# Folding a norm gain into a weight split and moving two pieces of work in a recurrent layer (HGRN) of a one-core kernel

## The reference, cut to what matters

```python
def hgrn2_mixer(h, w_in, lower_bound, out_norm, w_out, first_layer):
    q, f, i, g = jnp.split(h @ w_in, ..., axis=-1)     # four sections of 1024 columns
    q = jax.nn.silu(q)
    log_f = jax.nn.log_sigmoid(f32)                    # first layer
    k = -jnp.expm1(log_f)
    ...
    # by chunks of 64 tokens, each head: G = cumsum(log_f)
    #   attn[t, s] = sum_k q[t, k] * k[s, k] * exp(G[t, k] - G[s, k])   for s <= t
    #   o = attn @ i + (q * exp(G)) @ state
    o = rms_norm_2(o, out_norm) * jax.nn.silu(g.reshape(B, S, HGRN_HEADS, HGRN_DV).astype(jnp.float32))
    return o.reshape(B, S, HGRN_D_VAL).astype(h.dtype) @ w_out
```

## Time and profile before

| | us |
|---|---|
| median of 3 runs | 1095.07 |
| lowest, highest | 1093.2, 1097.18 |
| the profiled execution's own time | 1091.74 |
| its span | 1089.9 |
| PE, PEld busy | 1035.1 (95%), 847.1 (78%) |
| DVE, ACT, POOL busy | 780.1 (72%), 506.3 (46%), 111.9 (10%) |

### The profile page before, as it was taken

One profiled execution on the slowest core, in us unless ns is written; L12 is line 12 of the kernel. 1 busy time (PEld: TensorE's weight loads), 2 busy tenths in 40 slices (PEclk: granted clock), 3 DMA queues, 4 the chain that ended last, 5 costly groups with the idle time before them and its releaser, 6 DMA issues.

```text
span 1089.9 us, 16320 instructions
## 1 busy us (share of the span) xinstructions
PE 1035.1 (95%) x6217; PEld 847.1 (78%) x6217; DVE 780.1 (72%) x1023; ACT 506.3 (46%) x645; POOL 111.9 (10%) x137
## 2 busy tenths in 40 slices
PE   6998999999989999698999999999999989999998
PEld 5887777878867888587778888877878877888886
DVE  5776767786666878887898787788846786454554
ACT  5536364444544584453344343335547735443441
POOL 1000000000001000581300000000850200000000
PEclk9999999999999999899999999999999999999999
DMA  8975358698726977004399898954413064655641
GB/s 314 337 277 203 116 191 323 241 371 297 256 86 216 343 262 246 17 2 162 103 328 342 294 309 284 322 200 151 135 52 135 2 193 141 207 160 188 212 152 58
DMA packets 126959, 224.12 MB, mean 206 GB/s; under 512 B 4824, under 2 KB 58296, under 8 KB 126904
## 3 DMA queue, kind: packets, MB, share of 16 engines
q1 hardware_dynamic: 125936, 220.90, 58.0%
q0 software_dynamic: 656, 2.36, 0.8%
q10 hardware_dynamic: 312, 0.10, 0.0%
HBM read 222.30 MB, written 1.05 MB: 205 GB/s over the span
## 4 chain that ended last, share of the span: by engine, by line
PE 80%; DVE 13%; issue 3%; ACT 3%; DMA 1%; SPq 0%; POOL 0%; DVEq 0%; ACTq 0%; PEldq 0%
PE psum L1732 76%; DVE adaacc L1133 3%; DVE wlo L1107 2%; DVE arena L1174 2%; ACT whi L706 2%; PE psum L2372 1%; PE psum L2202 1%; DVE arena L1220 1%; DMA raw<-in_attn_w_qkv 1%; DVE arena L1435 1%; DVE gain_b L1435 1%; PE psum L2061 1%; DVE adaw L1382 1%; DVE res L1225 0%; PE psum L2289 0%
## 5 line engine op out<-in xcount | busy, mean ns | idle before, releaser
L1107 DVE TENSOR_TENSOR wlo<-raw,whi 128x2048 fp32r<-128x2048 f32 (+1 forms) x166 | 330.5, 2006 | 132.1 <-ACT whi L706 132.0
L1732 PE MATMUL psum<-whi,xhi 128*128 128x512 f32 x880 | 350.5, 398 | 11.3 <-DVE xlo L1182 10.4
L706 ACT CAST whi<-raw 128x2048 fp32r<-128x2048 f32 (+1 forms) x166 | 278.2, 1684 | 165.4 <-PE psum L1732 141.3
L1732 PE MATMUL psum<-whi,xlo 128*128 128x512 f32 x880 | 343.9, 391 | 0.0
L1732 PE MATMUL psum<-wlo,xhi 128*128 128x512 f32 x880 | 342.2, 390 | 0.0
L1732 PEld LDWEIGHTS psum<-whi,xhi 128*128 128x128 f32 x880 | 165.8, 188 | 47.8 <-issue 14.2
L1732 PEld LDWEIGHTS psum<-whi,xlo 128*128 128x128 f32 x880 | 165.6, 188 | 35.4
L1732 PEld LDWEIGHTS psum<-wlo,xhi 128*128 128x128 f32 x880 | 166.0, 189 | 32.3
L1133 DVE SCALAR_TENSOR_TENSOR adaacc<-adaw,cact,adaacc 128x512 f32<-128x512 f32 x196 | 147.3, 752 | 7.0 <-DMA adaw<-in_ada_w 0.2
L1732 PE MATMUL psum<-whi,hhi 128*128 128x512 f32 x304 | 120.2, 395 | 4.2 <-DVE wlo L1107 2.7
L1732 PE MATMUL psum<-whi,hlo 128*128 128x512 f32 x304 | 118.5, 390 | 0.0
(11 more groups left out here) (278 smaller groups left out, 1013.6 us busy)
## 6 DMA issues: line engine op xcount, KB each, us to landing
adaw<-in_ada_w SPq DMA_DIRECT2D x48, 1024.0 KB, 5.6
raw<-in_ffn_w_in SPq DMA_DIRECT2D x88, 512.0 KB
raw<-in_ffn_w_out SPq DMA_DIRECT2D x44, 512.0 KB
raw<-in_w_up SPq DMA_DIRECT2D x16, 1024.0 KB
raw<-in_w_down SPq DMA_DIRECT2D x16, 1024.0 KB
raw<-in_hgrn_w_in SPq DMA_DIRECT2D x16, 1024.0 KB
raw<-in_attn_w_qkv SPq DMA_DIRECT2D x12, 1024.0 KB
adaw<-in_kv_ada_w SPq DMA_DIRECT2D x8, 1024.0 KB, 6.8
```

The lines of the kernel that those rows point to most:

```text
L706: sc.copy(whi[:, s, 0:width], raw[:, s, 0:width]).then_inc(hi_ready[s], 1)
L1107: ve.tensor_tensor(wlo[:, s, 0:width], raw[:, s, 0:width], whi[:, s, 0:width].bitcast(F32), ALU.subtract).then_inc(lo_ready[s], 1)
L1732: return te.matmul(dst, lhsT, rhs, start=start, stop=stop, skip_group_check=open_)
```

## The change

Three edits, all in the HGRN layer.

1. The gain is no longer multiplied into the gate (`gains` and its two calls are gone). It is multiplied into the rows of `w_out`. A slot's partition p holds rows whose channel is p, so the gain is a column with one value for each partition: `onb`, now 128 x 1 in `stat`, loaded by a DMA of one column. For item `Q_HOUT` (four slots) ScalarE's high split is a multiply by this column and VectorE's low split is raw x column - high, one instruction of three operands. VectorE's and ScalarE's splits of this item wait for the column's DMA; VectorE's wait ahead of the heads is gone.
2. The diagonal sums move from the end of the projection into it: token tile 0 behind the third section's second eviction, tile 1 behind the fourth section's first eviction.
3. `outputs(HH - 1)` is called between part (0, 0) and part (0, 1) of the output projection.

```diff
-        onb = sb("onb", [P, DK])
+        onb = stat[:, 50:51]
...
-            gp.dma_start(onb[:], a["hgrn_out_norm_2"][0].partition_broadcast(P)).then_inc(norms_in, 16)
+            with nc.allow_non_contiguous_dma(reason="one column"):
+                gp.dma_start(onb, a["hgrn_out_norm_2"][0].rearrange("(p o) -> p o", o=1)).then_inc(norms_in, 16)
...
-                sc.copy(whi[:, s, 0:width], raw[:, s, 0:width]).then_inc(hi_ready[s], 1)
+                if isinstance(n, int) and n == Q_HOUT:
+                    act.wait_ge(norms_in, 16)
+                    sc.mul(whi[:, s, :], raw[:, s, :], onb).then_inc(hi_ready[s], 1)
+                else:
+                    sc.copy(whi[:, s, 0:width], raw[:, s, 0:width]).then_inc(hi_ready[s], 1)
...
-                ve.tensor_tensor(wlo[:, s, 0:width], raw[:, s, 0:width], whi[:, s, 0:width].bitcast(F32),
-                                 ALU.subtract).then_inc(lo_ready[s], 1)
+                if isinstance(n, int) and n == Q_HOUT:
+                    v.wait_ge(norms_in, 16)
+                    ve.scalar_tensor_tensor(wlo[:, s, :], raw[:, s, :], onb, whi[:, s, :].bitcast(F32), ALU.mult,
+                                            ALU.subtract).then_inc(lo_ready[s], 1)
+                else:
+                    ve.tensor_tensor(wlo[:, s, 0:width], raw[:, s, 0:width], whi[:, s, 0:width].bitcast(F32),
+                                     ALU.subtract).then_inc(lo_ready[s], 1)
...
-                        v.wait_ge(g_f, 2)
-                        for i in range(TT):
-                            chain(ve.tensor_tensor(qk, hin[:, 0, i, :], hk[:, i, :], ALU.mult))
-                            chain(ve.tensor_reduce(dg[:, i, :], qk.rearrange("p (h d) -> p h d", d=DK), AX, ALU.add))
                         q_part(0)
                     evac(Q_HIN + t, p, hin[:, sec, 1, p * 512:(p + 1) * 512])
+                    if (t, p) in ((N_HIN - 2, 1), (N_HIN - 1, 0)):
+                        i = t - (N_HIN - 2)
+                        v.wait_ge(g_f, 2)
+                        chain(ve.tensor_tensor(qk, hin[:, 0, i, :], hk[:, i, :], ALU.mult))
+                        chain(ve.tensor_reduce(dg[:, i, :], qk.rearrange("p (h d) -> p h d", d=DK), AX, ALU.add))
...
-            v.wait_ge(norms_in, 16)
...
-                    gains(4)
...
-                    gains(0)
...
                     part(0, 0)
+                    if second is not None:
+                        second()
                     part(0, 1)
...
-            outputs(HH - 1)
...
-            accumulate(Q_HOUT, 1, None, A_HOUT, 0, late_turn)
+            accumulate(Q_HOUT, 1, None, A_HOUT, 0, late_turn, second=lambda: outputs(HH - 1))
```

More of the change, by code:

```diff
@@ L1415, in gates_low @@
                                  ghi[:, :, b * 256:(b + 1) * 256].bitcast(F32), ALU.subtract).then_inc(g_lo, 1)
[L1417 to L1421, removed]
             def second(x, m):
@@ L1819, in project_tiles, with accumulate @@
                         project_part(n, 1, half, i, width)
-            def accumulate(n, turned, m=None, middle=None, gated=None, late=None, next_norm=None, early_high=False):
+            def accumulate(n, turned, m=None, middle=None, gated=None, late=None, next_norm=None, early_high=False, second=None):
                 def part(s, i):
```

## The result

The changed kernel took 1083.78 us (median of 4 runs, 1080.29 to 1084.53) against 1094.58 us (4 runs, 1093.2 to 1097.18): ratio 0.9894, interval 0.9873 to 0.9914. That is 10.8 us less; 11.4 were forecast. The profiled execution took 1084.53 us with a span of 1082.7, against 1089.9 before, a difference of only 7.2.

A forecast was written before the change was run, and what follows sets the result against it. The chain lies mostly on TensorE; in the HGRN layer, TensorE's waits for VectorE bound it. Terms 4.0 + 3.0 + 1.5 + 2.9 = 11.4 us took the median from 1095.07 to 1083.7, rounded to 1084; range 1080 to 1089.5.

The forecast's parts named there:

- Diagonal sums: End of the HGRN projection: pairs moved into VectorE's idle time let the first head's operand start 4.0 us earlier.
- the fold: Output-weight splits with the gain column: dearer VectorE splits cost the path 0.1 to 1.4 us, taken as 0.1.
- proportional price: VectorE's three-operand split: 752 ns for 512 elements scaled by length gives 3.01 us, 0.72 more per split.
- Gains: VectorE in the heads: removing the first gains call, slowed beside GpSimd, saves 3.0 us; the second call gives 0.
- Outputs: Last head: 12 projection matmuls before its output products remove TensorE's 1.50 us idle, so 1.5 us is gained.
- The last normed: VectorE's last normed, behind the last output products: 0.3 to 1.3 us later, with over 3 us to spare.
- The gate's weights: Weights for the gate after the output projection: if they land late, the outputs' gain is 0 to 1.5 us.
- Clock: TensorE in the heads: two slow-clock stretches vanish as idle shrinks, 1.35 + 1.55 = 2.9 us; bounds 0 and 4.2.
- The second stretch: TensorE at 462 to 468, granted clock 0.72, slowing scores and outputs: its removal gives 1.55 us.
- rival 2: Projection or head 1: one VectorE edit returns as a wait, 1089.1 or 1088.2 us; chance 0.10, both lost 0.05.
- rival 3: Heads, 440 to 490: TensorE stays at 1.2 GHz, 2 to 3 us per head, up to 1107.6; chance 0.03.
- Rival 1: Heads: the clock still falls, two stretches stay slow somewhere on the chain, 8.5 us gain remains, 1086.6; chance 0.20.

The follow-up runs named there:

- experiment 1: Kernel before with only the diagonal sums moved into the projection's third and fourth sections: 1089.22 us, ratio 0.995.
- experiment 2: Kernel before with only the output gain folded into the split of the output weights: 1092.52 us, ratio 0.9972.
- experiment 5: Kernel before with the first gains call cut to token tile 0, so heads 0 to 3 of tile 1 lack the gain: 1088.95 us, ratio 0.9958.
- experiment 3: Kernel before with only the last head's output products moved behind part (0, 0) of the output projection: 1092.65 us, ratio 0.998.
- experiment 4: Kernel before with 26 unread matmuls filling TensorE's idle time before head 1's exponents: 1092.93 us, ratio 0.9991.
- experiment 6: Changed kernel with 12 unread matmuls each before the last head's scores and the first MLP's modulation product: 1080.54 us, ratio to before 0.987.
- experiment 7: Changed kernel with both pairs of diagonal sums in the third section behind its second eviction: 1081.17 us, ratio to before 0.9876.
- experiment 8: Changed kernel with the edits of experiments 6 and 7 together: 1080.22 us, ratio to before 0.987.

## Why the prediction was right

**Diagonal sums: 4.0 forecast, 3.99 measured.** The hole before the third section's split took the first pair, as worked out; the first operand moved by 3.99 in the change and by 4.26 alone (experiment 1). So the fold's dearer instructions cost 0.27 us up to this operand, of which 0.09 are ScalarE's. The meeting of 4.0 and 3.99 is in part luck: without them the gain is 4.26, not 4.1, and they cost 0.27, not 0.1. The forecast took 0.1 out of bounds from 0.1 to 1.4; at the proportional price of 3.01 us per split, the term would have been 4.1 - 1.4 = 2.7. The row decides: 2.35 us per split.

**Gains: 3.0 forecast, 2.99 measured,** and 3.0 alone (experiment 2). That it is the slow price and not 1.28 is the point at which the forecast could have gone wrong by half, and experiment 5 shows what makes it slow. The call before the last head's pick brought nothing, as forecast: the pick of head 7 has gained no more than that of head 3.

**Outputs: 1.5 forecast, 1.52 measured,** 1.49 alone (experiment 3). The next matrix's first split keeps its 1.12 us wait for ScalarE and moved forward in full: it starts 10.88 us behind the last pick's start, before 12.40. The last normed kept its distance to that pick: it starts 7.51 us behind, before 7.44. The forecast had it 0.3 to 1.3 later. GpSimd's first step of the root (L570) does start 1.19 later behind the pick, but it takes 0.43 us instead of 1.55, and in both kernels it ends 0.05 or 0.06 us behind the end of VectorE's last split of the output weights. The gate's weights were not late.

**Clock: 2.9 forecast, 1.00 + 1.52 = 2.5 measured.** The second stretch gave 1.52 of 1.55. The first gave 1.37 on TensorE itself (442.14 to 444.13 is 1.99 us against 3.36), and experiment 4 gives 1.38 for it alone; but 0.35 was lost again on VectorE, whose operand starts 0.57 us behind the end of ScalarE's save, before 0.22. ScalarE's save before and after:

```profile
446.33 0.59 ACT L867 COPY adaacc<-psum 128x512 f32<-128x512 f32 x1 [0.79 <-PE psum L2104]
```

```profile
444.79 0.59 ACT L872 COPY adaacc<-psum 128x512 f32<-128x512 f32 x1 [0.29 <-PE psum L2108]
```

446.33 + 0.59 = 446.92, and the operand at 447.14; 444.79 + 0.59 = 445.38, and the operand at 445.95. The loss belongs to the fold and not to the clock: the wait is 0.57 to 0.58 us in all five kernels that have the fold (the change, experiments 2, 6, 7 and 8) and 0.22 to 0.23 in the five that don't (before, experiments 1, 3, 4 and 5), at low clock and at full. Whether the wait for the column that was taken out ahead of the heads makes it, or something else in the fold, is open. So the fold gave 3.0 and cost 0.27 + 0.35 = 0.6 on this path, where the forecast had 0.1.

**The sum.** 4.0 + 1.0 + 3.0 + 1.5 + 1.5 = 11.0 in the layer against 11.4 forecast, and 10.8 between the medians. That the forecast median (1083.7) meets the measured one (1083.78) to 0.1 us is luck: the saving is 0.6 smaller than forecast, and the kernel before came out 0.5 lower in four runs (1094.58) than in the three that the forecast starts from (1095.07). The edits' single gains are 6.2, 2.9 and 2.75 us between medians, 11.8 together, and 5.5, 3.1 and 2.2 by the ratios, 10.7 together, so they add up within their intervals. Fold and outputs may lean on each other slightly, as the fold alone leaves a larger gap before the last outputs (2.04 us), which the new order fills.

**Rivals.** Of rival 2 (an edit comes back as a wait) only the 0.35 us above are seen, and of rival 3 (the heads all slow) nothing: the first operand and head 2's scores wait no longer than forecast, and the heads between run at full clock. Rival 1 was right in its mechanism outside the place where it was looked for: low clock did appear at 170 to 177, where the change has no instruction, and costs 3.2 us in the profiled execution. The profiled executions of experiments 1, 2 and 4 have it too, those of the kernel before and of experiments 3, 5 and 7 don't, so it follows none of the three edits. I take it for part of the spread of the medians and not for a price of the change. That one kernel shows it in some executions and not in others is likely from that, but not shown, since each has one profile. Inside the layer, too, single profiles miss the sum of their terms: in experiment 2 the terms give 3.0 and 1.5, and 2.81 is measured.

## What to carry to other kernels

Put small work of the bounding chain into the hole that the profile shows in front of an instruction waiting for another engine, and price it by that hole: 2.5 us in a hole of 3.1 cost nothing. Before you price a VectorE instruction that is to go, look at what GpSimd does beside it and at what the next instruction waits for: the call that took 2.96 us beside GpSimd's multiply was worth 3.0, and its twin of 1.28 us, with a wait for TensorE behind it, nothing. Then look for the price of what replaces it at the next hand-over between engines too: 0.35 of the fold's 0.6 us stood there and in no instruction's own time. When a few microseconds are at stake, read each term between two near marks of the trace, since low clock elsewhere moved the whole span by 3 us.

## What the runs showed of the hardware that was not expected

- The same idle time of 2.21 us of TensorE before the same instruction was followed by full clock in one execution and by 0.54 in another. Of the eight kernels in which it is not filled, four have low clock behind it in their profiled execution (the change, experiments 1, 2 and 4). The other four (before, experiments 3, 5 and 7) have it at 86 to 92 instead (0.50 to 0.61 in 88 to 90), where the first four have full clock. The program is the same at both places. One execution each can't show what decides it.
- Filling one gap can uncover the next: in experiment 4 the gain of 1.38 us behind the first gap was given back behind later ones that had been there all along.
- A column of 128 values costs little: VectorE's split of 128x2048 takes 2.34 to 2.35 us with it and 2.29 without, ScalarE's high half 2.01 to 2.03 us against 1.91 to 1.92. The 752 ns of three operands for 512 elements doesn't grow in proportion.
- GpSimd's short step of the root, on 4 values a partition, took 0.35 to 1.55 us in the profiles of all ten kernels. In each it started while VectorE's split of 128x2048, with two SBUF inputs, was running, and ended 0.05 to 0.06 us behind it: here VectorE came first, and GpSimd seems to be the one that was held.
